# Last group of a mixture of experts outside the loop: weights in halves, results ahead of roundings, residual in PSUM

## What is computed

```python
x = x + hybrid_mixer(rms_norm(x, attn_norm), ...)
h = rms_norm(x, ffn_norm)
# router: softmax over 8 groups, one group per token (weight g_w), in it the best 2 of 8 experts
def expert_block(xb, e):                     # 64 experts: w1, w3 [1024, 512], w2 [512, 1024]
    return (silu(xb @ w1[e]) * (xb @ w3[e])) @ w2[e]
x = x + sum_over_chosen_experts(gate * expert_block(h, e))
return rms_norm(x, final_norm)
```

## Time and profile before

| | us |
|---|---|
| median of 3 runs | 1821.52 (1821.43 to 1821.63) |
| profiled execution, its own time | 1819.25 |
| its span | 1817.5 |
| last group, PE's first matmul | 1694.36 |
| last unit's rounding starts | 1792.10 |
| last matmul of the last unit ends | 1805.4 |
| last output DMA issued | 1814.5 |

### The profile page before, as it was taken

The page is one execution under the profiler, slowest core; times in us unless marked ns, Lnnn a source line. Parts: engine busy times, 40 slices in busy tenths (PEclk is TensorE's granted clock), DMA queues, the critical chain, the costliest instruction groups (busy, mean ns, idle before and its releaser), DMA issues.

```text
span 1817.5 us, 25124 instructions
## 1 busy us (share of the span) xinstructions
PE 1739.9 (96%) x9700; PEld 1483.9 (82%) x9700; DVE 1578.2 (87%) x1372; ACT 1219.7 (67%) x949; POOL 127.5 (7%) x140
## 2 busy tenths in 40 slices
PE   8999999999999999999999999999999999999997
PEld 7977888889888889988877877778777787778775
DVE  5787778789677776677999999999999999999997
ACT  5465454443333355446788988889888898888985
POOL 1255000000000010540000000000000000000000
PEclk9999999999999999999999999999999999999999
DMA  7521345553345556226799999999999999999994
GB/s 287 193 93 70 140 181 200 213 238 140 134 179 189 193 202 227 94 105 254 310 428 428 427 429 429 428 428 428 429 428 428 429 429 428 428 429 428 428 429 198
DMA packets 40647, 544.16 MB, mean 299 GB/s; under 512 B 4624, under 2 KB 4752, under 8 KB 5904
## 3 DMA queue, kind: packets, MB, share of 16 engines
q1 hardware_dynamic: 40592, 543.39, 72.7%
HBM read 542.33 MB, written 1.05 MB: 299 GB/s over the span
## 4 chain that ended last, share of the span: by engine, by line
PE 63%; DMA 13%; issue 5%; ACT 5%; DVE 4%; POOL 0%; DVEq 0%; ACTq 0%; POOLq 0%; SPq 0%
PE psum L1455 19%; DMA ring<-in_w 13%; PE psum L1003 9%; PE psum L852 7%; PE psum L1020 7%; PE psum L1005 4%; PE psum L1469 4%; ACT arena_r L1866 4%; PE psum L1484 2%; PE psum L895 2%; DVE ring_r L2392 1%; PE psum L1219 1%; PE psum L912 1%; PE psum L1393 1%; PE psum L1357 1%
## 5 line engine op out<-in xcount | busy, mean ns | idle before, releaser
L2392 DVE TENSOR_TENSOR ring_r<-ring,arena_r 128x4096 fp32r<-128x4096 f32 x192 | 847.7, 4425 | 16.0 <-ACT arena_r L1866 12.7
L1866 ACT ACTIVATE arena_r<-ring 128x4096 fp32r<-128x4096 f32 x188 | 682.2, 3629 | 61.8 <-DMA ring<-in_w 61.3
L1455 PE MATMUL psum<-arena_r,stream_r 128*128 128x512 f32 x1024 | 410.7, 401 | 11.0 <-DVE stream_r L2482 9.2
L1455 PE MATMUL psum<-ring_r,stream_r 128*128 128x512 f32 x1024 | 403.2, 394 | 0.0
L1003 PE MATMUL psum<-stream_r,arena_r 128*128 128x512 f32 x704 | 250.4, 398 | 2.0 <-DVE stream_r L1952 1.7
L1455 PEld LDWEIGHTS psum<-arena_r,stream_r 128*128 128x128 f32 x1024 | 194.9, 190 | 55.8 <-DVE ring_r L2392 11.3
L1653 ACT ACTIVATE arena_r<-ring 128x3072 fp32r<-128x3072 f32 x40 | 111.1, 2776 | 181.0 <-DMA ring<-in_ffn 181.0
L1455 PEld LDWEIGHTS psum<-ring_r,stream_r 128*128 128x128 f32 x1024 | 194.9, 190 | 39.0
L1005 PE MATMUL psum<-stream_r,ring_r 128*128 128x256 f32 x704 | 197.4, 280 | 0.0
L1484 PE MATMUL psum<-arena_r 128*128 128x512 f32 x512 | 161.2, 396 | 11.6 <-DVE arena_r L2541 10.8
L852 PE MATMUL psum<-stream_r,ring_r 128*128 128x256 f32 x968 | 167.3, 284 | 0.0
(11 more groups left out here) (336 smaller groups left out, 2483.8 us busy)
## 6 DMA issues: line engine op xcount, KB each, us to landing
ring<-in_w SPq DMA_DIRECT2D x192, 2048.0 KB, 12.8
ring<-in_ffn SPq DMA_DIRECT2D x44, 1536.0 KB, 6.3
ring<-in_w_in SPq DMA_DIRECT2D x8, 2048.0 KB, 7.9
ring<-in_in_w SPq DMA_DIRECT2D x7, 2048.0 KB, 12.7
ring<-in_out_w SPq DMA_DIRECT2D x7, 2048.0 KB, 7.9
ring<-in_l_in SPq DMA_DIRECT2D x8, 1536.0 KB, 8.7
ring<-in_proj SPq DMA_DIRECT2D x2, 2048.0 KB, 8.0
ring<-in_misc SPq DMA_DIRECT2D x1, 1632.0 KB, 8.5
```

Source lines behind the costliest of these rows:

```text
L1455: last = mm(dst, xg[:, k, :], b[:, k * D_EXPERT:(k + 1) * D_EXPERT], start=(k == 0 and b is u_hi), stop=(k == KD - 1 and b is u_lo))
L1866: A(w_hi[u % HI_SLOTS], ring[:, MOE_SLOT[at], :], ACT.Copy).then_inc(m_hi, 1)
L2392: V.tensor_tensor(ring_r[MOE_SLOT[u % NM]][:, :], raw, w_hi[u % HI_SLOTS].bitcast(F32), ALU.subtract).then_inc(m_lo, 1)
```

## The change

1. **The loop covers 7 groups; the last group's code stands behind it**, written out once more, without the work for a next group (`select`, `gather`).
2. **Halves.** From unit 6 of the last group, each unit comes as two DMAs of 1 MB (`rest_in_halves`), is rounded in two copies of 128x2048 (`halves_hi`), gets its remainder in two (`halves_lo`), and TensorE starts on the first half (`m_lo_half`) and waits for the second (`m_lo`).
3. **Order of the last group.** Up to unit 11 a rounding is still done 4 units ahead and a remainder 3 ahead. From `AHEAD_FROM` = 12 both are done 2 ahead and behind the results due at u. Nothing is rounded at u = 8 and 9.
4. **Residual in banks.** TensorE multiplies `x` by the identity into the four banks (`residual_in_bank`, at u = 8, 10, 12 and 20), and `send_last` adds to them. `add_back` is gone for the last group.
5. **Last unit by columns.** Its second half is multiplied for the column half 0 first, then (`m_y_half`) for 1, so that `y_hi`, `y_lo`, and the sending back go by column half.
6. **Last norm from PSUM.** Four square sums over 512 columns, read from the banks; POOL adds two for each tc; DVE multiplies by the gain ahead of the root for one quarter and ACT scales it; three output DMAs.

```diff
+        N_HALVED = NM - SLOTS
+        HALF = [slice(0, SLOT // 2), slice(SLOT // 2, SLOT)]
+        AHEAD_FROM = 12
+        LAST_BANK = (2, 3, 7, 0)
+        BY_HALF = [(tc, h) for h in range(2) for tc in range(NT)]
...
+            def rest_in_halves(n, g8, p):
+                for u in range(SLOTS, NM):
+                    kind, e = MOE[u]
+                    slot = MOE_SLOT[u]
+                    sp.wait_ge(m_unit, n * NM + (u - SLOTS + 1))
+                    for at, half_in in zip(HALF, (half_landed[slot], landed[slot])):
+                        sp.dma_start(ring[:, slot, at], d[kind][g8 + e][:, at]).then_inc(half_in, 16)
...
+            sp.wait_ge(out_ready, 2)
+            sp.dma_start(out[0:P, :], x[:, 0, :]).then_inc(out_sent, 16)
+            sp.wait_ge(out_ready, 3)
+            sp.dma_start(out[P:2 * P, 512:1024], x[:, 1, 512:1024]).then_inc(out_sent, 16)
+            sp.wait_ge(out_scaled, 1)
+            sp.dma_start(out[P:2 * P, 0:512], x[:, 1, 0:512]).then_inc(out_sent, 16)
...
             def expert_out(u, n, p=None):
+                halved = p is not None and u >= SLOTS
...
+                for j in range(NE // 2 if halved else NE):
                     for b in (u_hi, u_lo):
                         for h in range(2):
+                            last = product(j, b, h)
+                if halved:
+                    pe.wait_ge(m_lo, n * NM + (u + 1))
+                    for h in range(2):
+                        for j in range(NE // 2, NE):
+                            for b in (u_hi, u_lo):
+                                last = product(j, b, h)
+                        if u == NM - 1 and h == 0:
+                            last.then_inc(m_y_half, 1)
...
+            def residual_in_bank(i):
+                tc, h = RES[i]
+                mm(psum[:, LAST_BANK[i], :], ident, x[:, tc, h * 512:(h + 1) * 512], start=True, stop=False,
+                   skip_group_check=True)
+            def send_last(n):
+                for h in range(2):
+                    for part_y, ready in ((y_hi, (m_y_hi, 2 * n + (h + 1))), (y_lo, (m_y_lo, 2 * n + (h + 2)))):
+                        pe.wait_ge(*ready)
+                        for tc in range(NT):
+                            last = mm(psum[:, LAST_BANK[2 * tc + h], :], sel_gT[:, tc * P:(tc + 1) * P],
+                                      part_y[:, h * 512:(h + 1) * 512], start=False, stop=(part_y is y_lo),
+                                      skip_group_check=True)
+                            if part_y is y_lo:
+                                last.then_inc(m_sc, 1)
...
         @block.scalar
...
+            def halves_hi(u, n, p):
+                act.wait_ge(half_landed[slot], p * (16 * (PER_SLOT - 1)) + 16 * (u // SLOTS))
+                act.wait_ge(m_unit, n * NM + (u - HI_SLOTS + 1))
+                A(w_hi[u % HI_SLOTS][:, HALF[0]], ring[:, slot, HALF[0]], ACT.Copy).then_inc(m_hi_half, 1)
+                act.wait_ge(landed[slot], n * (16 * PER_SLOT) + (MOE_BASE[at] + 16 * (u // SLOTS + 1)))
+                A(w_hi[u % HI_SLOTS][:, HALF[1]], ring[:, slot, HALF[1]], ACT.Copy).then_inc(m_hi, 1)
...
+                for u in range(NM):
+                    results(u, n)
+                    if u + HI_SLOTS < SLOTS:
+                        split_hi(u + HI_SLOTS, n)
+                    elif u + HI_SLOTS < AHEAD_FROM:
+                        halves_hi(u + HI_SLOTS, n, p)
+                    if AHEAD_FROM <= u + 2 < NM:
+                        halves_hi(u + 2, n, p)
+                act.wait_ge(m_y_half, p + 1)
+                result_hi(0)
+                act.wait_ge(m_unit, n * NM + NM)
+                result_hi(1)
...
+            for i, (tc, h) in enumerate(RES):
+                act.wait_ge(m_sc, n + (BY_HALF.index((tc, h)) + 1))
+                A(xn[:, tc, h * 512:(h + 1) * 512], psum[:, LAST_BANK[i], :], ACT.Square,
+                  accum_out=last_ss[:, tc, h:h + 1]).then_inc(squares, 1)
+            act.wait_ge(x_gained, 1)
+            act.wait_ge(rstd_ready, NT * NORMS["last"] + 2)
+            A(x[:, 1, 0:512], h_raw[:, 0, 0, :], ACT.Copy, scale=rstd[:, NORMS["last"], 1:2]).then_inc(out_scaled, 1)
...
         @block.vector
...
+                for u in range(NM):
+                    if u + 3 < SLOTS:
+                        split_lo(u + 3, n)
+                    elif u + 3 < AHEAD_FROM:
+                        halves_lo(u + 3, n, p)
+                    hidden(u, n)
+                    if u == SEND_AT:
+                        add_back(n)
...
+                    if AHEAD_FROM <= u + 2 < NM:
+                        halves_lo(u + 2, n, p)
+                for i in range(2):
+                    result_lo(i, n)
...
+            last = NORMS["last"]
+            dve.wait_ge(row_in, 48)
+            dve.wait_ge(squares, NT * last + 3)
+            V.tensor_tensor(h_raw[:, 0, 0, :], psum[:, LAST_BANK[2], :], norm_row[:, 0:512], ALU.mult).then_inc(x_gained, 1)
+            for tc, h in ((0, 0), (0, 1), (1, 1)):
+                at = slice(h * 512, (h + 1) * 512)
+                dve.wait_ge(rstd_ready, NT * last + tc + 1)
+                V.scalar_tensor_tensor(x[:, tc, at], psum[:, LAST_BANK[2 * tc + h], :], rstd[:, last, tc:tc + 1],
+                                       norm_row[:, at], ALU.mult, ALU.mult).then_inc(out_ready, 1)
```

211 lines of the change are left out of this document (128 added, 83 removed).

## The result

The changed kernel takes **1824.19 us** (median of 20 runs, 1822.97 to 1827.83), the kernel before 1820.43 beside it (20 runs, 1819.07 to 1823.74): a ratio of 1.002, 95% interval 1.0014 to 1.0026. That is 3.8 us slower; 3.3 were forecast. The profiled execution took 1826.97 us, its span is 1825.1. In what follows, medians and ratios leave out two executions of `ahead18` in a slower state (1908.71 and 9773.02 us); no other run had one.

A forecast was written before the change was run, and what follows sets the result against it. Weight transfers at 428 GB/s set the last landing, with DVE full beside them. The last remainder at 1809.7 plus 11.2 gives 1820.9 against a 1817.5 span; 1821.5 + 3.3 = 1824.8 us, range 1818 to 1829.

The forecast's parts named there:

- rounding of unit 12 starts: ACT, last group: starts at 1746.15 behind unit 10's results instead of 1739.11, so seven us of lead are given away.
- loop over a fold: Last group: unit u, fold, silu, rounding of u+2, remainders and matmuls take 10.6 us from unit u to u+2.
- 12 to 23: Last group: from unit 12 multiplied to unit 23 multiplied, four loops over folds and three DVE-bound steps, 57.1 us.
- F: End of the last remainder on DVE: 1796.4 if engines followed landings, 1809.7 with the new order; 1800.2 before.
- F to the end: Last matmuls, sending back, norm and output behind the last remainder: 11.2 us, against 17.3 before.
- four loops: Last group's path over folds, units 12-14, 15-17, 18-20 and 20-22, at 10.6 us each: 42.5 us.
- The open price: New end: POOL's last mean beside DVE's gain and scaling could delay root 1 by 0 to 0.9 us; taken as 0.
- The looser loop: Rival, last group: DVE never idles again from unit 12's first half at 1748.1; time 1819.2; chance 0.13.
- the engines in step: Rival, last group: engines keep step with the landings, 9.9 us gained, time 1812; chance 0.08.
- The clock: Rival, TensorE in the loops: half clock makes one loop 14.4 us, a stretch costs up to 3.4, 1828; chance 0.14.
- the fourth rival: Rival, transfers: 1 MB DMAs are slower, 1.4 us each, last landing 25 us later, time 1837; chance 0.03.
- the 9.9 of the landings: Whole span: 9.9 us earlier, ending at 1807.6, if the last remainder followed the last landing; not believed.

The follow-up runs named there:

- ahead18: Changed kernel with the switch to the new order at unit 18 instead of 12, for ACT and DVE; 1822.37 us, kernel before 1821.17, ratio 1.0007.
- corner runs: Changed kernel with the order alone undone (1818.46 us), with order and halves undone (1818.22 us), and with halves alone undone (1855.13 us).
- best16_out2: Changed kernel with units whole up to 15, order switched at unit 20 (ACT) and 21 (DVE), two output DMAs instead of three; 1816.36 us, ratio 0.9979.
- order_whole: Changed kernel with its new order and new end, but whole units instead of halves; 1855.13 us, kernel before 1821.43, ratio 1.0184.
- order_whole_busy: Changed kernel with whole units, plus four unread float32 products ahead of units 12, 14, 16, 18, 20 and 22; 1844.27 us, ratio 1.0129.
- whole_dma: Changed kernel with one 2 MB DMA per unit, roundings, remainders and matmuls still in halves; 1824.95 us, kernel before 1820.56, ratio 1.0021.
- all_dma_halves: Kernel before with all 192 units loaded as two 1 MB DMAs instead of one of 2 MB; 1834.14 us, kernel before 1821.17, ratio 1.0078.

## Why the prediction was right

**By its own steps**, with times of the changed kernel less 3.44:

| step | predicted | measured |
|---|---|---|
| remainder of unit 11 ends | 1744.1 | 1744.16 |
| rounding of unit 12 starts | 1746.15 | 1746.17 |
| half rounding, half remainder | 1.94, 2.29 | 1.91, 2.29 |
| unit 12 multiplied | 1754.7 | 1754.77 |
| loop over a fold (18 to 20) | 10.6 | 10.64 |
| 12 to 23 | 57.1 | 57.2 |
| F | 1809.7 | 1809.78 |
| F to the end | 11.2 | 11.9 |
| clock in the loops | 1.00 (rival: half) | 1.00 |

Up to F the steps were right, and the corner runs show that they were right for the stated reason: with the order undone, and halves, residual and end left in, the loss becomes a gain. Two things in it are luck. The first of the four loops was not the one I had summed: it went by unit 13 and a residual product, and came out 0.05 us off because the two ways are nearly equal there. And the forecast of 1824.8 stands closer to 1824.19 than its working deserves: it starts from 1821.5, the median of 3 runs, where 20 runs have 1820.43. The fair comparison is +3.3 with +3.8, and the end accounts for the difference.

**The term that was mis-sized is the end**, by 0.7 us. The sums' copies and the four banks came as costed: `y_lo` of the half 0 ends at F + 2.61 (2.6), the banks are done at F + 4.33 (4.3). The four square sums are quicker: they start 0.57 apart, not 0.73, and are done at F + 5.88 instead of 6.25. POOL takes 1.30 from the last of them to the root, not 1.0: when the third square sum was ready (1818.52) it was still at the first root (until 1819.12), so that three steps, 0.19, 0.26 and 0.55, are left to do for the second. DVE's last scaling ends at F + 8.16 (8.0), the last issue stands at F + 8.57 (8.4), and from it to the end are 3.3 us (2.8). I had bounded this term by the 3.0 us of two DMAs of 512 KB issued 2.1 us apart; as the third of three issued within 1.1 us it takes more, and taking one issue away (best16_out2) gives nothing clear back.

**The open price was 0**, as taken: the POOL operation that had taken 1.07 us beside DVE's scaling takes 0.26 beside DVE's L2708, which reads one operand from PSUM, and 0.27 with DVE idle (at 1818.22). The rule of the Trainium skill (SBUF — State Buffer, "Who interferes with whom") agrees with both rows: it lets a DVE instruction contend with GpSimd when two of its inputs come from SBUF, and not when at most one does. No run here changes the operand alone.

**The rivals.** The looser loop and the engines in step did not occur: ACT has no wait for a DMA from unit 6 on. The clock did not occur in the changed kernel; order_whole shows what it would have taken: with whole units TensorE waits 3.4 to 5.4 us instead of 0.9 at most, and it costs 11 us. At waits in between, up to 1.31 us in order_whole_busy and 1.58 in ahead18, the clock stays at 1.00; between 1.6 and 3.4 us the last group has none in the traces read for this. The transfers in halves are slower, by 0.07 us a unit and not by 1.4, and here they hide: the transfers end near 1797.7, 2 to 3 us later than before on its scale, and the last rounding starts at 1805.95, some 8 us later still. So the last landing had moved, by a tenth of what the fourth rival gives; whole_dma shows that this costs nothing in this order.

**What I had not seen.** That without the new order the end would be bound by TensorE (three units, a fold and a residual product back to back), so that keeping the lead gives 3 us and not the 9.9 of the landings; that 1.3 us of the old end were a wait for hidden values; and that the new order may be right over the last four units. In sum, on the scale of before, F comes 9.6 us later (1800.2, 1809.78) and the end is 5.4 us shorter (17.3, 11.9): 4.2, the difference of the last stretches.

## What to carry to other kernels

In engines that work through a list in order, moving a result ahead of the work done in advance helps only where that work has slack; count first who is ahead of whom, and by how much, at the unit where the order switches. Put the switch where the bound changes hands: at unit 12 of 24 it lost 6.4 us, at unit 18 it still lost some 4, and over the last four units it was at the least no loss. And split into halves where something waits for the first half: in the new order that was worth 30 us, with the lead kept it neither gained nor cost.

## What the runs showed of the hardware

- **TensorE came back from idle time at half clock** (order_whole). In six units behind 3.4 to 5.4 us without a matmul, 6 to 14 of the 16 matmuls stood 0.43 us apart, at a granted clock of 0.50 where a window shows them alone, and the unit took 5.1 to 6.6 us instead of 3.7; after up to 1.6 us (ahead18, 1.58 before 1780.03) it kept 1.00. Useless float32 matmuls in the idle time made the kernel 11 us faster (order_whole_busy).
- **DMA size in a full queue.** 1 MB: 422 GB/s (all_dma_halves); 2 MB: 428 (before); over 192 units this makes 13 us.
- **The last landing.** The program ends 3.3 to 3.4 us after the issue of 256 KB as the third DMA in a queue, 3.7 after 512 KB as the second, and in both cases 4.35 to 4.45 us after the issue of the first; a lone median from issue to landing (2.6) does not tell the end.
- **Executions stand up to 4.4 us apart at the same instruction** of the last group (the mark lies between 1708.67 and 1713.04 in the versions that load the first seven groups alike), in code that none of them touches. Single spans can't show 2 us; a stretch from a common mark came to within 1.5 us of the differences that the ratios give.
